# One block from the gated product to the last MLP, the keys' turns moved into the first MLP's end, and the output product begun in the last attention head

## What is computed

```python
y = s5_mixer_states(x)                       # state-space mixer, gelu
y = glu(y @ w_glu) @ w_out                   # gated product: a * sigmoid(b), then the output product
x = layer_norm(ALPHA * x + y)
x = layer_norm(ALPHA * x + relu(x @ w1)**2 @ w2)      # first MLP, 4096 wide
ckv = rms_norm(x @ kv_w_a);  cq = rms_norm(x @ q_w_a) # latents, 256 and 384 wide
k = ckv @ kv_w_b;  q = cq @ q_w_b                     # 8 heads, 128 + 64 (rotary) wide
o = attention(q, k, v, causal) @ w_o
x = layer_norm(x + o)
x = layer_norm(ALPHA * x + relu(x @ w1)**2 @ w2)      # second MLP
```

## Time and profile before

| | us |
|---|---|
| median of three runs | 3354.71 (3354.69, 3354.71, 3359.87) |
| the profiled execution, whole | 3359.43 |
| its span | 3357.3 |
| PE busy in the span | 3240.8 (97%) |
| DVE, ACT, POOL busy | 1576.7, 869.2, 1207.2 |
| mean granted TensorE clock | 0.985 of full |
| DMA, mean of the span | 52 GB/s |

### The profile page before, as it was taken

One profiled execution on the slowest core, in us unless ns is written; L12 is line 12 of the kernel. 1 busy time (PEld: TensorE's weight loads), 2 busy tenths in 40 slices (PEclk: granted clock), 3 DMA queues, 4 the chain that ended last, 5 costly groups with the idle time before them and its releaser, 6 DMA issues. The chain is left out here.

```text
span 3357.3 us, 49162 instructions
## 1 busy us (share of the span) xinstructions
PE 3240.8 (97%) x19620; PEld 2828.8 (84%) x19620; DVE 1576.7 (47%) x3043; ACT 869.2 (26%) x1685; POOL 1207.2 (36%) x953
## 2 busy tenths in 40 slices
PE   8999999989989899999999999989999999999998
PEld 7898989879988788888888888978889888888886
DVE  4647464634579412443333334555552533333335
ACT  3545454541113211211111111544331311111111
POOL 5434343314139233643333332411104633333232
PEclk9999999979999999999999999999999999999999
DMA  6211102043001211121111111000002111111111
GB/s 190 71 53 47 54 28 71 15 163 86 32 17 23 58 48 41 63 76 50 50 50 50 50 50 35 7 17 19 17 20 89 51 51 50 48 40 50 50 38 51
DMA packets 180099, 173.28 MB, mean 52 GB/s; under 512 B 50043, under 2 KB 162875, under 8 KB 179771
## 3 DMA queue, kind: packets, MB, share of 16 engines
q1 hardware_dynamic: 179838, 170.72, 16.1%
q10 hardware_dynamic: 96, 0.26, 0.0%
HBM read 156.97 MB, written 19.23 MB: 52 GB/s over the span
## 5 line engine op out<-in xcount | busy, mean ns | idle before, releaser
L2489 DVE TENSOR_TENSOR x<-x,banks 128x512 f32<-128x512 f32 x508 | 342.5, 686 | 216.1 <-PE banks L80 216.1
L78 PE MATMUL banks<-winbuf_hi,xt_hi 128*128 128x256 f32 x1024 | 302.0, 295 | 12.1 <-ACT qkn L855 7.5
L80 PE MATMUL banks<-winbuf_hi,xt_lo 128*128 128x256 f32 x1024 | 290.3, 284 | 0.0
L79 PE MATMUL banks<-winbuf_lo,xt_hi 128*128 128x256 f32 x1024 | 290.2, 283 | 0.0
L78 PEld LDWEIGHTS banks<-winbuf_hi,xt_hi 128*128 128x128 f32 x1024 | 196.5, 192 | 31.3 <-ACT qkn L855 11.5
L277 POOL CAST f2w_buf_hi<-f2w_raw 128x2048 fp32r<-128x2048 f32 x32 | 61.2, 1914 | 403.3 <-PE banks L80 403.3
L277 POOL CAST f1w_buf_hi<-f1w_raw 128x2048 fp32r<-128x2048 f32 x32 | 61.2, 1913 | 403.3 <-PE banks L80 403.3
L78 PE MATMUL banks<-h1t_hi,f1w_buf_hi 128*128 128x512 f32 x512 | 199.6, 390 | 1.6 <-issue 1.6
L78 PE MATMUL banks<-h3t_hi,f2w_buf_hi 128*128 128x512 f32 x512 | 199.4, 390 | 1.6 <-issue 1.6
L78 PE MATMUL banks<-f2w_buf_hi,f2a_hi 128*128 128x512 f32 x512 | 199.3, 389 | 1.4 <-DVE f2a_lo L2479 1.4
L80 PE MATMUL banks<-f1w_buf_hi,f1a_lo 128*128 128x512 f32 x512 | 199.3, 389 | 0.0
(11 more groups left out here) (461 smaller groups left out, 8417.6 us busy)
## 6 DMA issues: line engine op xcount, KB each, us to landing
f1w_raw<-in_w_ff SPq DMA_DIRECT2D x32, 1024.0 KB, 5.1
f2w_raw<-in_w_ff SPq DMA_DIRECT2D x32, 1024.0 KB, 5.1
winraw<-in_w_in SPq DMA_DIRECT2D x128, 128.0 KB, 3.3
gluw_raw<-in_ssm_w_glu SPq DMA_DIRECT2D x14, 512.0 KB, 4.3
x<-in_x SPq DMA_DIRECT2D x8, 512.0 KB, 6.3
wow_raw<-in_w_out SPq DMA_DIRECT2D x4, 1024.0 KB, 5.9
x<-in_x SPq DMA_DIRECT2D x1, 4096.0 KB, 14.9
gew_raw<-in_w_ple_gate SPq DMA_DIRECT2D x4, 1024.0 KB, 5.0
```

What stands on the lines that cost most here:

```text
L78: nc.tensor.matmul(out, a.hi, b.hi, start=start, stop=False)
L79: nc.tensor.matmul(out, a.hi, b.lo, start=False, stop=False)
L80: return nc.tensor.matmul(out, a.lo, b.hi, start=False, stop=stop)
L2489: nc.vector.tensor_tensor(xx, xx, chip.ps[:, bank, :], ALU.add).then_inc(s_acc, 1)
```

## The change

- `stage_glu`, both `stage_mlp` and `stage_attention` share one block, so three block ends go. A stage's work waits by name instead: `Ready` lists the semaphores that the next product's loads, its splits and the two halves of its rows wait for.
- The `recycle` ahead of `stage_attention` goes, and the one ahead of `stage_s5` moves behind it, ahead of the gated product.
- The split of the first gated chunk on POOL also waits for the last `hs` of S5.
- Transposing the key latent and the rotation tables, and what ACT and DVE do with them, moves from the head of attention into the tail of the first MLP, between the turns of tiles 4 to 7. PE's first `keys` now waits for the low parts of the keys and of all the turned tiles.
- In the last head PE does seven of eight contraction steps of the output product's first four tiles (`Product.begin`), two of them ahead of the rounds' ends for t = 6 and 7, one behind the last product with the values, one behind the last turned rows.
- The values are released to DVE in four parts, and DVE copies parts 2 and 3 ahead of its round t = 0.
- The norm's two statistics semaphores become one, and all streams share one semaphore `held`.

```diff
-            dve.wait_ge(self.aggr, j - 1)
+            dve.wait_ge(self.stat, 3 * (j - 1))
...
+class Ready:
...
+    def __init__(self, loads, splits, first_half, second_half):
+        self.loads, self.splits, self.halves = loads, splits, (first_half, second_half)
...
+def wait_all(eng, waits):
+    for sem, value in waits:
+        eng.wait_ge(sem, value)
...
 class Product:
...
+        wait_all(pool, self.ready.splits)
...
+    def step(self, j, k):
+        return mm3(self.nc, self.chip.ps[:, j, 0:CH], self.rows.at(slice(None), k, slice(j * P, j * P + P)),
+                   self.ws.bufs[0].at(slice(None), k, slice(None)), k == 0, k == KT - 1)
...
+    def begin(self, pe, j):
...
+        if j == 0:
+            pe.wait_ge(self.ws.split, 1)
+        for k in range(KT - 1):
+            self.step(j, k)
+        self.begun = j + 1
...
-                self.tile(ps[:, j, 0:CH], n, n, j).then_inc(self.mm, 1)
+                elif j % 4 == 0:
+                    wait_all(pe, self.ready.halves[j // 4])
+                if n == 0 and j < self.begun:
+                    self.step(j, KT - 1).then_inc(self.mm, 1)
+                else:
+                    self.tile(ps[:, j, 0:CH], n, n, j).then_inc(self.mm, 1)
...
-            then.split_ahead(pool)
+            then.split_ahead(pool, (s_h, 4 * NB))
...
+        pool.wait_ge(done[0], done[1])
...
+        return Ready([(s_mm, 2 * KT)], [(s_mm, 2 * KT)], [(s_lo, 2 * KT + 1)], [(s_lo, 2 * KT + 2)])
...
+            wait_all(sp, product.ready.loads)
...
-            for j in range(4, NT):
-                latent.turn(pe, j)
+            latent.turn(pe, 4)
+            latent.turn(pe, 5)
+            latent.turn_keys(pe, 0)
+            latent.turn(pe, 6)
+            latent.turn_keys(pe, 1)
+            latent.turn(pe, 7)
+            latent.turn_rotors(pe)
...
-            for j in range(4, NT):
-                latent.high(act, j)
+            latent.high(act, 4)
+            latent.high(act, 5)
+            latent.keys_high(act, 0)
+            latent.high(act, 6)
+            latent.keys_high(act, 1)
+            latent.high(act, 7)
+            latent.waves_out(act)
...
+            latent.rotors(dve)
...
+            latent.keys_low(dve, 0)
...
+            latent.keys_low(dve, 1)
+            latent.low(dve, 7)
...
+    def turn_keys(self, pe, half):
...
+        pe.wait_ge(self.scaled[0], 4 * half + 4)
+        if half:
+            pe.wait_ge(self.scaled[1], NT)
+            pe.wait_ge(self.rt_done, 4 * NT)
+        for k in range(KV_LORA // P):
+            for j in range(4):
+                last = self.nc.tensor.transpose(self.banked(2 * half + k)[:, j, :],
+                                                self.c[0][:, 4 * half + j, k * P:(k + 1) * P], self.chip.ident[:, :])
...
+    def keys_high(self, act, half):
+        for k in range(KV_LORA // P):
+            act.wait_ge(self.key_turned, 2 * half + k + 1)
+            act.wait_ge(self.made[1], NT)
+            self.nc.scalar.activation(self.by_token(self.ckvt.hi[:, k, :], half), self.banked(2 * half + k), ACT.Copy,
...
+    def keys_low(self, dve, half):
+        for k in range(KV_LORA // P):
+            dve.wait_ge(self.key_highs, 2 * half + k + 1)
+            hi, lo = (self.by_token(t[:, k, :], half) for t in (self.ckvt.hi, self.ckvt.lo))
+            self.nc.vector.scalar_tensor_tensor(lo, self.banked(2 * half + k), self.gains[:, k:k + 1], f32(hi),
+                                                ALU.mult, ALU.subtract).then_inc(self.key_lows, 1)
...
+    def rotors(self, dve):
+        dve.wait_ge(self.made[1], NT)
+        for m, (wave, by) in enumerate(((self.cos, 1.0), (self.cos, 1.0), (self.sin, -1.0), (self.sin, 1.0))):
+            self.nc.vector.tensor_scalar(self.rotor[:, :, m, :], wave[:, :, :], by, None, ALU.mult).then_inc(self.rotor_made, 1)
+        for n in range(2):
+            self.nc.vector.tensor_tensor(self.fold[:, n * ROPE:(n + 1) * ROPE], self.chip.ident[:, 0:ROPE],
+                                         self.chip.ident[:, ROPE:P], ALU.add).then_inc(self.folded, 1)
...
+    def turn_rotors(self, pe):
+        pe.wait_ge(self.rotor_made, 4)
+        pe.wait_ge(self.lows, 4 * 6)
+        for half in range(2):
+            for j in range(4):
+                last = self.nc.tensor.transpose(self.banked(4 + half)[:, j, :],
+                                                self.rotor[:, 4 * half + j, :, :].rearrange("p a r -> p (a r)"),
+                                                self.chip.ident[:, :])
+            last.then_inc(self.rotor_turned, 1)
...
+    def waves_out(self, act):
+        for n in range(2):
+            act.wait_ge(self.rotor_turned, n + 1)
+            for half in range(2):
+                self.nc.scalar.activation(self.by_token(self.wave[half][:, :], n),
+                                          self.banked(4 + n)[:, :, half * 64:half * 64 + 64],
...
+            sp.wait_ge(latent.turned, NT)
...
+            pool.wait_ge(latent.made[1], NT)
...
-                last.then_inc(s_v, 1)
+                    if t % 2:
+                        last.then_inc(s_v, 1)
...
-            pe.wait_ge(s_clo, 4)
+            pe.wait_ge(latent.key_lows, 4)
+            pe.wait_ge(latent.lows, 4 * NT)
             for half in range(2):
                 keys(0, half)
             pe.wait_ge(s_round, 2)
-            pe.wait_ge(s_fold, 2)
-            pe.wait_ge(s_turn, 4)
+            pe.wait_ge(latent.folded, 2)
+            pe.wait_ge(latent.wave_out, 4)
...
+                    else:
+                        product.begin(pe, t + 2 - NT)
...
+            product.begin(pe, 2)
             turn_rows(N_HEADS - 1, NT - 1)
+            product.begin(pe, 3)
...
+                if h == 0:
+                    dve.wait_ge(latent.wave_out, 4)
...
-                dve.wait_ge(s_v, 2 * p + n // 2 + 1)
+                dve.wait_ge(s_v, 4 * p + n + 1)
...
+                if h % 2 == 0:
+                    value_copy(h // 2, 2)
+                    value_copy(h // 2, 3)
...
-                    if t in (1, 2) and h % 2 == 0:
-                        value_copy(h // 2, 1 + t)
...
+        done = [(s_ol, NT * N_HEADS + NT)]
+        return Ready([(s_o, NT * N_HEADS)], [(s_sc, NT * N_HEADS)], done, done)
...
-        recycle(nc)
...
+        recycle(nc, keep=(ws.landed, ws.hi, ws.split))
...
+        block = ctx.enter_context(nc.Block())
+        gated = stage_glu(nc, block, chip, ws, y5, y5t, gt, so)
...
-        recycle(nc, keep=(heads.landed, heads.hi, heads.split))
```

## The result

| | before | after |
|---|---|---|
| first comparison: median, us | 3357.29 (3354.71, 3359.87, 3354.69, 3360.03) | 3335.70 (3325.07, 3335.09, 3336.88, 3336.31) |
| ratio | | 0.9932, 95% interval 0.9914 to 0.9950 |
| second comparison: median, us | 3358.62 (eleven runs, 3347.55 to 3363.07) | 3336.98 (six runs, 3325.05 to 3343.72) |
| ratio | | 0.9934, 95% interval 0.9913 to 0.9955 |
| PE busy in the span | 3240.8 of 3357.3 | 3222.3 of 3323.3 |

The forecast was 3338.0 with a range of 3330 to 3347. The time is 3335.7 and in the second comparison 3337.0, some 21.6 us or 0.64% under before.

The account below looks back on a forecast made before the run. PE, busy 97% of the span, was taken as the bound, so gains come only from its stops or half-rate stretches. Terms -1.7 + 0.7 - 5.9 - 1.8 - 3.4 - 4.9 = -17.0 us gave 3338, range 3330 to 3347.

Parts of the forecast that it names:

- A: Seam ahead of S5: removing `recycle` there gives -1.7 us.
- B: End of S5: earlier outputs -3.3, moved `recycle` +1.7, half-rate gated product start +2.3; +0.7 us, from -3.1 to +1.2.
- rival 1: The stops go but the half-rate clock keeps its toll, there or elsewhere: -11.5 us, 3343, chance 0.19.
- C: Gated product to output product: stop of 3.29 us and half-rate stretch of 2.6 go; -5.9 us, at least -3.3.
- D: First MLP to attention: `keys` 4.3 us sooner, half-rate clock costs 2.5; -1.8 us, from -4.3 to -1.0.
- E: Values in attention: PE's eight waits for them go; -3.4 us, from 0 to -3.6.
- F: Last head: four stops of 3.3 us and a half-rate stretch costing 1.6 go; -4.9 us, from -3.3 to -5.5.
- The base: The time before from which the predicted gain was subtracted: the median of the runs, 3354.71 us.
- Rival 2: `hs` gives everything back and the clock stays kind: -23.9 us, 3331, chance 0.10.
- Rivals 3 and 4: Changed parts fail to do what they say: 3349, chance 0.06; instructions come late, kernel slower: 3364, chance 0.03.

Follow-up runs that it names:

- a_nowait: The changed kernel, but POOL's split of the first gated chunk no longer waits for the last `hs` of S5: 3340.97 us.
- a_nobegin: The changed kernel without the four `product.begin` calls in the last head, so the whole output product is made behind it: 3339.10 us.
- b_wait: The kernel before, with only the wait of POOL's split for the last `hs` of S5 added: 3352.84 us.
- a_best: The changed kernel with unused identity transposes in three PE stops and attention's wait for all low parts moved behind the first `keys`: median 3330.21 us, ratio 0.9921 to before.
- a_values: The changed kernel with value copies 2 and 3 put back into DVE's rounds t = 1 and t = 2: 3343.28 us.
- b_pieces: The kernel before, with POOL's subtraction of 2048 columns cut into four of 512 and no added wait: 3359.0 us.
- after_again: The changed kernel, unaltered, run again in the second comparison: median 3336.98 us, ratio 0.9934 to before.

## Why the prediction was right, and where it was not

**A** was right: -1.75 (predicted -1.7), and +1.74 when `recycle` was put back.

**B** came to -3.60 + 1.46 + 1.74 + 1.15 = +0.75, predicted +0.7, but in part by luck. The first step held: POOL blocked DVE, and `tm` is late next. The `recycle` held too. The toll at the gated product's start was sized too high, at 2.3: its half-rate stretch is some 3.2 us long (0.52 from 1114.76 to 1118.00) and costs 1.15 (183.11 less 181.96 with the clock kept). And I left to the low end that the stretch behind `outputs` might go. The stop there halved from 7.2 to 3.5 us, and the half-rate stretch grew from 3.0 us to at least 5.7: +1.46. The stop's length didn't set it. `a_nowait`, with its stop of 7.2, took 8.52 us to the last gelu, but so did `a_nobegin` (8.54) with a stop of 3.9. These two also began the gated product at full clock, 181.9 us ahead of the output product, behind the same 3.3 us stop as the others. What decides between the two is open; rival 1's premise, that the clock takes its toll in another place, was true here, but not its sum.

**C** was right: the table's -2.28 holds B's +1.15, so C is -3.43 - 2.58 = -6.0 (-5.9), and 5.3 of it came back with the block's end. The 2.58 depends on the execution of before that it is counted from: `b_wait`, with the same code and the same block end there, took 47.65 us to the 512-column part and not 48.65, its clock being back at 1.00 from 1315.4 us. So about 1 us of C is the profiled execution's.

**D** was right in its chain (its bound of -1.0 doesn't follow from its own terms, which give -4.3 + 2.8 = -1.5), -4.29 against -4.3, and the clock took +2.08 of the +2.5 given: -2.2 in place of -1.8. 30 to 40 transposes ahead of `keys` gave that back.

**E and F** are where the sum was mis-sized: -5.54 and -5.81, not -3.4 and -4.9. The term that failed is the same in both: I took a stop for its recorded idle. By `a_values` eight stops of 3.6 us in all cost 5.57, and by `a_nobegin` four of 3.2 cost 4.16: each costs about a quarter of a microsecond more than its bracket (0.25 and 0.24). F's half-rate stretch was rightly sized, 1.67 against 1.6, but the prediction took it for certain, and of three profiles of before's code there, before and `b_pieces` have it and `b_wait` does not (79.4 us and not 80.9): some 1.5 us of F belong to the profiled execution. The terms were sized from one trace, and that trace can't say how often a half-rate stretch comes.

**S5's rounds** were given nothing, and took 129.0 us in place of 130.2. `a_nobegin`, `a_nowait` and `a_best`, with the same code there, took 130.2 to 130.6, so this 1.2 us isn't the edit. It goes with the clock: before has it at 0.50 from 1017.7 to 1021.0 us with PE busy throughout, the second profile of the changed kernel at 1.00 from 1014 to 1025, and the three kernels just named have 3 us at 0.50 near the same place (from 1017.7, 1014.9 and 1012.9 us). That makes the clock the likely cause; no run tests it.

**The base** was off the other way. The gain is 21.6 us and not 17; but the median of before is 3357.3 to 3358.6 with more runs, not the 3354.71 of three. From 3358.62, a sum of -21.6 gives 3337.0. The forecast of 3338 is that near by luck: two errors of some 4 us cancel, the gain of 21.6 taken as 17 and the median of before taken some 4 us too low. Nor is the table's -21.9 exact for the edits: S5's 1.2 us and the parts of C and F named above, 3.7 in all, are of the two executions compared.

Rival 2 named nearly the right gain (-23.9) for partly wrong reasons: it had B at -3.1 and D at -4.3, which the clock refused. Rivals 3 and 4 have nothing for them: the split of chunk 1 kept 4.0 us of cover, and no wait between heads appeared.

## What to carry to other kernels

Price the removal of a stop by the distance between the starts of the instructions on both sides of it, against the same pair without a stop, and not by the recorded idle; with many short stops the difference is as large as the gain. Where a stop can't be removed, fill it with matrix work of no use, ahead of the wait: 74 transposes in three stops gave 5.8 us in one profile here (the ten at the gated product kept the clock in one profile of three), and 58 in a stage that the change doesn't touch gave 11.3 us there by the profiles. Before a half-rate stretch is priced, look for it in a second execution. When an elementwise operation waits out one of another engine, order the two; cutting the long one in four pieces only spread the loss here.

## What the runs showed of the hardware

- DVE's operations with two operands in SBUF slow down beside POOL in S5's middle rounds as well, not only at its end. Timeline of the kernel before, a middle round:

```profile
1059.50 1.61 POOL L1791 TENSOR_TENSOR pwtmp<-c,a_difference 128x576 f32<-128x576 f32 x1
1061.08 1.61 POOL L1791 TENSOR_TENSOR pwtmp<-c,a_powers 128x576 f32<-128x576 f32 x1
1062.83 3.03 POOL L1796 TENSOR_TENSOR q<-pwtmp,pwtmp 128x576 f32<-128x576 f32 x2
...
1060.01 1.65 DVE L2014 TENSOR_TENSOR hs<-ht,rot 128x508 f32<-128x508 f32 x1
1061.58 1.65 DVE L2015 SCALAR_TENSOR_TENSOR hs<-ht,rot 128x508 f32<-128x508 f32 x1
1063.26 0.69 DVE L1978 TENSOR_TENSOR s5tmp<-banks,rot 128x512 f32<-128x512 f32 x1
```

  `hs` takes 1.65 us, the pace of POOL's 1.61, and 0.68 when POOL is still; with one operand in PSUM (`banks`) it is 0.69 beside POOL as well. The rule of the Trainium skill that the prediction cites, that the second of two such operations is blocked in full, agrees with `a_nowait` (4.81 us) and also with `b_pieces`: with many operations on both sides each is blocked for one of the other's.
- The same code behind the same stop of 3.3 us ran at full clock in two profiles and at half for some 3 us in others (181.9 and 183.0 to 183.2 us to the output product). Behind attention, with the same four stops, it was at 0.50 for 3.2 us in before and at 1.00 in `b_wait`. In the first mixer the clock stayed at 0.50 from 705 to 740 us, across stops of 0.7 to 2.7 us, in the profiles of before and `after_again`, and that makes some 12 us against the profiles in which it came back sooner. It is probably most of the spread between runs: 3347.6 to 3363.1 for before, 3326.0 to 3334.6 in `a_best`, and 3312.9 to 3317.4 with the mixer's stops filled as well.
- Clearing semaphores isn't free: the same `recycle` behind S5 took 0.9 us less when another had been ahead of S5, with 0.15 us of clearing on POOL in place of 0.76.
